# A two-layer trunk in fp32 halves: three RMS norms drawn into the stages behind them

## What is computed

```python
def rmsnorm(x, g, eps=1e-6):
    xf = x.astype(F32)
    y = xf * lax.rsqrt(jnp.mean(xf * xf, axis=-1, keepdims=True) + eps)
    return (y * g.astype(F32)).astype(x.dtype)

def mlstm_mixer(h, w_in, ...):
    proj = h @ w_in                      # q, k, v, o of 16 heads of 128, and two gates
    ...
    return (jax.nn.sigmoid(o) * hc) @ w_out

def peer(h, w_q, sub_k1, sub_k2, u, v):
    q = jnp.einsum('bsd,dhk->bshk', h, w_q)       # 8 heads, two sides of 128
    s1 = jnp.einsum('bshk,hnk->bshn', q1, sub_k1)
    s2 = jnp.einsum('bshk,hnk->bshn', q2, sub_k2)
    # top 16 of each side, top 16 of their 256 sums, softmax: expert numbers and gates
    # act = gelu(u[idx] . h) * gate;  out = sum act * v[idx]

for i in range(2):
    x = x + mixer(rmsnorm(x, norm_mix[i]))
    x = x + peer(rmsnorm(x, norm_ffn[i]), ...)
    x = x + sigmoid(rmsnorm(x, norm_ple[i]) @ ple_gate[i]) * (p[i] @ ple_w[i])
```

## Time and profile before

| | us |
|---|---|
| median of 3 runs | 4439.07 (4438.66 to 4439.1) |
| the profiled execution | 4438.94 |
| its span in the trace | 4437.4 |
| mean granted clock of TensorE over the span | 0.982 |
| TensorE, VectorE, ScalarE, GpSimd busy in it | 4265.6, 2664.8, 2108.6, 1237.8 |

### The profile page before, as it was taken

One profiled execution on the slowest core, in us unless ns is written; L12 is line 12 of the kernel. 1 busy time (PEld: TensorE's weight loads), 2 busy tenths in 40 slices (PEclk: granted clock), 3 DMA queues, 4 the chain that ended last, 5 costly groups with the idle time before them and its releaser, 6 DMA issues. The chain is left out here.

```text
span 4437.4 us, 61663 instructions
## 1 busy us (share of the span) xinstructions
PE 4265.6 (96%) x19295; PEld 3448.9 (78%) x19295; DVE 2664.8 (60%) x5626; ACT 2108.6 (48%) x4073; POOL 1237.8 (28%) x1571
## 2 busy tenths in 40 slices
PE   6999899999999999999799998999999999999997
PEld 5765687888888888887588886888888888888884
DVE  3546489777774444444577763887777744444444
ACT  2755343677773333333355552434778743333323
POOL 0210145777870000000100000446888810000000
PEclk9999999999999999999899999999999999999998
DMA  2111233555557565652122222335555575555531
GB/s 101 58 48 38 86 111 123 190 200 184 201 207 256 182 211 172 209 173 81 62 86 87 85 82 81 111 116 173 204 179 203 184 282 174 207 186 197 196 112 57
DMA packets 178192, 653.90 MB, mean 147 GB/s; under 512 B 17200, under 2 KB 17328, under 8 KB 172928
## 3 DMA queue, kind: packets, MB, share of 16 engines
q1 hardware_dynamic: 100944, 371.41, 25.3%
q0 software_dynamic: 40240, 213.69, 13.6%
q10 hardware_dynamic: 36864, 67.13, 4.0%
HBM read 507.42 MB, written 144.74 MB: 147 GB/s over the span
## 5 line engine op out<-in xcount | busy, mean ns | idle before, releaser
L184 PE MATMUL ps<-h_hi,w_hi 128*128 128x512 f32 x4296 | 1692.1, 394 | 102.6 <-PEq L280 51.9
L184 PE MATMUL ps<-h_lo,w_hi 128*128 128x512 f32 x4296 | 1678.8, 391 | 0.0
L184 PE MATMUL ps<-h_hi,w_lo 128*128 128x512 f32 x4296 | 1678.5, 391 | 0.0
L163 DVE TENSOR_TENSOR w_lo<-w_raw,w_hi 128x1024 fp32r<-128x1024 f32 x585 | 719.0, 1229 | 1060.9 <-ACT w_hi L157 1056.3
L157 ACT ACTIVATE w_hi<-w_raw 128x1024 fp32r<-128x1024 f32 x694 | 734.8, 1059 | 904.2 <-PE ps L184 731.2
L184 PEld LDWEIGHTS ps<-h_hi,w_hi 128*128 128x128 f32 x4296 | 809.7, 188 | 282.0 <-issue 90.6
L184 PEld LDWEIGHTS ps<-h_hi,w_lo 128*128 128x128 f32 x4296 | 809.5, 188 | 171.8
L184 PEld LDWEIGHTS ps<-h_lo,w_hi 128*128 128x128 f32 x4296 | 810.1, 189 | 159.5 <-issue 0.2
L1481 POOL TENSOR_SCALAR second_hot<-iota,token_keys 128x128 fp32r<-128x128 f32 x1024 | 723.4, 721 | 0.0
L1519 ACT ACTIVATE first_scaled<-first_hot,token_keys 128x128 fp32r<-128x128 f32 x1792 | 539.3, 387 | 0.4 <-DVE first_scaled L1451 0.4
L170 POOL TENSOR_TENSOR w_lo<-w_raw,w_hi 128x1024 fp32r<-128x1024 f32 x109 | 283.2, 2599 | 706.8 <-ACT w_hi L157 706.8
(11 more groups left out here) (308 smaller groups left out, 3515.0 us busy)
## 6 DMA issues: line engine op xcount, KB each, us to landing
w_raw<-in_u SPq DMA_DIRECT2D x256, 512.0 KB, 3.6
w_raw<-in_v SPq DMA_DIRECT2D x256, 512.0 KB, 3.5
gates<-gate_group POOLq DMA_DIRECT2D x36, 2048.0 KB, 7.9
acts<-gelu ACTq DMA_DIRECT2D x256, 256.0 KB, 2.2
gate_block<-gates POOLq DMA_DIRECT2D x32, 2048.0 KB, 18.1
gelu_block<-acts POOLq DMA_DIRECT2D x30, 2048.0 KB, 11.7
w_raw<-in_od_in SPq DMA_DIRECT2D x65, 512.0 KB, 3.5
w_raw<-in_ev_in SPq DMA_DIRECT2D x33, 512.0 KB, 3.5
```

Source lines behind the costliest of these rows:

```text
L163: self.nc.vector.tensor_tensor(self.wl[:, slot % SPL, :], self.raw[:, slot, :], self.wh[:, slot % SPL, :].bitcast(F32), ALU.subtract).then ...
L184: ins = self.nc.tensor.matmul(out, a[:, s, w], b[:, k, :], start=first and j == 0 and m == 0, stop=last and j == n - 1 and m == 2)
```

## The change

A class `Norm` takes the place of `norm` ahead of the three stages. ScalarE rounds `x * gain` tile by tile into a high half and squares `x`; VectorE makes the low half from `x * gain`; both go into a pair of halves of their own. TensorE makes the stage's first product on these halves as they come, with the sum of squares of a tile one tile behind (`pe_unit`). Root and reciprocal follow. The block of `norm` and one barrier are gone, and the stage's SyncE and GpSimd start while the norm is at work.

In `TopK` the pair is `y_hi`/`y_lo`. The first four query products run on it, in a row, and VectorE multiplies the factor in as it evicts them (`peer_q`, now four slots). In between VectorE makes the normalised tiles, and ScalarE and VectorE their halves `h_hi`/`h_lo`, for all other products; the first product of `u` waits for them tile by tile. The first units are thus four of wq; from then on each step is a product of `u`, the query four ahead and the scores two ahead, in a loop of three passes of four steps.

In the odd mixer the pair is `h_hi`/`h_lo`, and all products run on it; the factor is multiplied in where k, q, v and the gates are evicted (a copy becomes a multiplication). The o product is now evicted by VectorE with the factor (`taken_o`, between `low` and `weigh`), and the sigmoid works in place on SBUF. ScalarE's split of the unit for v is moved behind the logarithm. Some gate rows share buffers.

```diff
+class Norm:
+    def act_tile(self, act, k):
+        a.activation(self.hi[:, k, :], p.x[:, k, :], ACT.Copy, scale=p.col(self.gain, k)).then_inc(self.nh.sem, 1)
+        if k >= 2:
+            act.wait_ge(self.ss.sem, self.ss.at(k - 1))
+        a.activation(self.s2[:, k % 2, :], p.x[:, k, :], ACT.Square).then_inc(self.sq.sem, 1)
+    def act_root(self, act):
+        act.wait_ge(self.ss.sem, self.ss.at(DK))
+        a.activation(self.rstd, ps[:, self.bank, :], ACT.Copy, scale=1.0 / (DK * P), bias=EPS).then_inc(self.ro.sem, 1)
+        act.wait_ge(self.ro.sem, self.ro.at(1))
+        a.activation(self.rstd, self.rstd, ACT.Sqrt).then_inc(self.ro.sem, 1)
+    def dve_tile(self, dve, k):
+        dve.wait_ge(self.nh.sem, self.nh.at(k + 1))
+        p.nc.vector.scalar_tensor_tensor(out=self.lo[:, k, :], in0=p.x[:, k, :], scalar=p.col(self.gain, k),
+                                         in1=self.hi[:, k, :].bitcast(F32), op0=ALU.mult, op1=ALU.subtract
+                                         ).then_inc(self.nl.sem, 1)
+    def pe_unit(self, pe, u, out):
+        def tile(k):
+            if k:
+                self.pe_sum(pe, k - 1)
+            pe.wait_ge(self.nl.sem, self.nl.at(k + 1))
+        p.product(pe, u, u % RAW, out, self.hi, self.lo, wait_tile=tile).then_inc(p.sig("w_used").sem, 1)
+        self.pe_sum(pe, DK - 1)
...
 class TopK:
     def tensor(self, pe):
+        self.norm.pe_unit(pe, u0, p.ps[:, 4, :])
+        for n in range(1, L):
+            query(u0 + n, (u0 + n) % RAW, 4 + n, (p.yh, p.yl))
+        pe.wait_ge(sl.sem, sl.at(16))
+        for n in range(2):
+            scores(n, None, n, n)
+        def body(n, c, i):
+            u, at = i * 8 + u0 + L + 2 * c, u0 + L + 2 * c
+            if c < 1:
+                rows.multiply(pe, n, c % 2, u, at % RAW, lambda k: pe.wait_ge(self.sll.sem, self.sll.at(k + 1)))
+            else:
+                rows.multiply(pe, n, c % 2, u, at % RAW)
+            pe.wait_ge(qt.sem, n + qt.base + 3)
+            query(u + 1, (at + 1) % RAW, 4 + c % 2, (p.hh, p.hl))
+            scores(n + 2, n + 2, (c + 2) % L, c % 2)
     def scalar(self, act):
+        for k in range(DK):
+            self.norm.act_tile(act, k)
+            if k == 3:
+                split(1)
+        self.norm.act_root(act)
+        split(2)
+        for k in range(DK):
+            act.wait_ge(self.sf.sem, self.sf.at(k + 1))
+            a.activation(p.hh[:, k, :], self.hf[:, k % 2, :], ACT.Copy).then_inc(self.sh.sem, 1)
+            if k == 1:
+                split(3)
+            if k == 5:
+                split(4)
+        split(5)
     def vector(self, dve):
+        self.norm.dve_root(dve)
+        query(0)
+        for k in range(DK):
+            v.scalar_tensor_tensor(out=self.hf[:, k % 2, :], in0=p.x[:, k, :], scalar=p.col(self.norm.gain, k),
+                                   in1=rstd, op0=ALU.mult, op1=ALU.mult).then_inc(self.sf.sem, 1)
+            if k:
+                low(k - 1)
+            if k in (0, 3, 7):
+                query((0, 3, 7).index(k) + 1)
+        low(DK - 1)
...
 class OddMixer:
     def scalar(self, act):
         def sigmoid(n):
-            act.wait_ge(used.sem, n * 4 + h0 + 4)
-            a.activation(self.os[:, :], p.ps[:, 1, :], ACT.Sigmoid).then_inc(self.sg.sem, 1)
+            act.wait_ge(self.ot.sem, n + self.ot.base + 1)
+            a.activation(self.os[:, :], self.os[:, :], ACT.Sigmoid).then_inc(self.sg.sem, 1)
     def vector(self, dve):
-            v.tensor_copy(qk[:, j, CONV - 1:], p.ps[:, j, :]).then_inc(self.taken.sem, 1)
+            v.tensor_tensor(qk[:, j, CONV - 1:], p.ps[:, j, :], rstd, ALU.mult).then_inc(self.taken.sem, 1)
...
+        def taken_o(n):
+            dve.wait_ge(used.sem, n * 4 + h0 + 4)
+            v.tensor_tensor(self.os[:, :], p.ps[:, 1, :], rstd, ALU.mult).then_inc(self.ot.sem, 1)
...
             low(n, half, i)
+            taken_o(n)
             weigh(n)
```

More of the change, by code:

```diff
@@ L1165, in tensor, with scores @@
-        for j in range(4):
-            rows.multiply(pe, 2 * H + j, j % 2, u0 + 4 * H + j, (u0 + j) % RAW)
+        def scores(n, key, slot, s):
+            pe.wait_ge(qt.sem, n + qt.base + 1)
+            if key is not None:
+                pe.wait_ge(stk.sem, n + stk.base + 1)
+            sub = self.subk[:, n, :] if key is None else self.subk[:, bass.ds(key, 1), :].rearrange("p o k -> p (o k)")
+            for t in range(TT):
+                ins = p.nc.tensor.matmul(p.ps[:, 2 + s, t * KEYS:(t + 1) * KEYS],
+                                         self.qf[:, slot, t * P:(t + 1) * P], sub, start=True, stop=True)
+            ins.then_inc(sr.sem, 1)
@@ L1168, in scalar @@
+        self.loop(pe, body)
+        for m in range(4 * H - L, self.N):
+            n = m - 2 * H
+            rows.multiply(pe, n, n % 2, u0 + m, (u0 + m) % RAW)
+            if n + 2 < 2 * H:
+                scores(n + 2, n + 2, (n + 2) % L, n % 2)
     def scalar(self, act):
-        p, u0, rows, H = self.p, self.u0, self.rows, PEER_HEADS
+        p, u0, rows, H, L = self.p, self.u0, self.rows, PEER_HEADS, self.LEAD
         qt, sr, stk, tf, used = self.qt, self.sr, self.stk, self.tf, p.sig("w_used")
+        a = p.nc.scalar
@@ L1193, in gpsimd @@
+        self.loop(act, body)
+        for m in range(4 * H - L, self.N):
+            n = m - 2 * H
+            if m + 2 <= self.N:
+                split(m + 2)
+            rows.gelu(act, n, n // 2, n % 2, u0 + m)
+            if n + 2 < 2 * H:
+                copy(n + 2, n % 2)
     def gpsimd(self, pool):
```

172 lines of the change are left out of this document (107 added, 65 removed).

## The result

The changed kernel takes **4398.37 us** (median of 4 runs, 4395.7 to 4400.38); the kernel before took 4439.09 beside it. The ratio is 0.9907, 95% interval 0.989 to 0.9924. The profiled execution took 4396.69 us, its span is 4395.2 (before 4437.4), its mean granted clock 0.987 (before 0.982). The prediction was 4396.1 us.

The account below looks back on a forecast made before the run. TensorE, busy 96% of the span, bounds the kernel; only its stand-still or half clock can be won. Peer layers -16.6 and -15.6, odd mixer start -15.6, decode +2, head loop +3: -42.8 us, 4438.9 to 4396.1 us; range 4384 to 4410.

## What to carry to other kernels

Before an operation is added to a loop, look for the wait that ends last in it: the first 0.68 us on VectorE cost 0.17 us a head, since 0.5 us of slack stood there, 0.34 of it a wait that the timeline shows; the next cost 0.71. When a stage starts behind a barrier, count TensorE's stand-still from the last matmul of the stage before to the first of the new one, and fill it with matmuls nobody reads, up to about 1.5 us from the start; here closing the last 3 us down to 1.2 to 1.6 gave 5 us. Look at the barrier behind the filling: ahead of the second peer layer it came 1.0 us later. Two causes of one wait may each be enough to lift it when removed: an experiment that removes one and succeeds has not cleared the other.

## What the runs showed of the hardware that I had not expected

- The same code took 476.07 us to its first peer layer in one execution and 480.00 in another, by a granted clock of 0.79 or 0.70 between 300 and 340 us. A stand-still of TensorE of a given length is not always followed by the same stretch of half clock. In the decode stage, too, TensorE stood for 2.11 us in the changed kernel and for 2.10 in the kernel with the first low weight on VectorE; the busy table from 704 to 725 us of the one and then of the other:

```profile
704.00:725.00 21.00, 18.89 (x83) 15.09 (x82) 20.73 (x12) 8.18 (x9) 13.02 (x5) 1.00 0.33 112
```

```profile
704.00:725.00 21.00, 18.90 (x77) 15.16 (x76) 20.72 (x21) 8.75 (x10) 12.38 (x4) 0.92 0.32 110
```

  The kernel before stood 3.10 us there with 1.00 from 716 to 740 us. With the old kernel's pauses filled, two stand-stills of 2.5 us were followed by 1.00 and by 0.70. So the length alone doesn't settle it.
- At the starts of stages half clock followed wherever TensorE had stood for 2.9 to 4.3 us, and none where it had stood for 1.2 or 1.6 us; at 2.5 us both were seen. A filled pause kept the clock at 1.00 even where the pause was 17 us.
- ScalarE's copy with a scale per partition took 0.71 us where the plain copy of the same shape took 0.63; back to back with a square both hide 0.1 us, so the pair cost 1.14 us (predicted 1.3).
- A multiplication on VectorE beside GpSimd's weight subtraction took 2.72 to 2.75 us against 0.74. In the case shown above it ended at 507.10, 0.54 us after GpSimd's subtraction of 2.54 us had (506.56): GpSimd's remaining 2.2 us account for the 2.0 us of difference. It happened twice at the first peer layer's start.
